# First mixture of a two-block kernel: one gather for two experts, results spread by 32-row strips, and layer one's further passes behind its whole first pass

## The reference, cut to what matters

```
logits = h @ w_router + b_router
top_v, top_e = top_k(logits, 4);  weights = softmax(top_v)
# for each expert e, with the tokens routed to it:
hcat  = x[tok] @ w1[e] + b1[e]                  # 1024 -> 2048
x_glu = min(hcat[:, ::2], 7);  x_lin = clip(hcat[:, 1::2], -7, 7)
act   = x_glu * sigmoid(1.702 * x_glu) * (x_lin + 1)
y     = act @ w2[e] + b2[e]                     # 1024 -> 1024
out[tok] += weights[tok, e] * y
```

## Time and profile before

| what | us |
|---|---|
| median of 3 runs | 2179.35 |
| the runs | 2178.27 to 2183.54 |
| span of the profiled execution, core 0 | 2180.7 |
| first mixture in it: first layer one to the last sum | 392.4 to 1397.5 |
| tensor engine busy | 1818.2 (83%) |

### The profile page before, as it was taken

How to read it: one execution, slowest core, us unless ns; L and a number is a source line. 1 busy time by engine, 2 the same in 40 slices (tenths; PEclk the granted TensorE clock), 3 DMA queues, 4 the chain that set the end, 5 groups by cost and what they waited for, 6 DMA issues and landing times. The chain is left out here.

```text
span 2180.7 us, 28331 instructions
## 1 busy us (share of the span) xinstructions
PE 1818.2 (83%) x11496; PEld 831.2 (38%) x11496; DVE 806.8 (37%) x1613; ACT 506.2 (23%) x1028; POOL 77.0 (4%) x96
## 2 busy tenths in 40 slices
PE   7899999999999988989977898599989855565556
PEld 3654445433333433434333243255534522222221
DVE  2215533333342434534444344488882200000001
ACT  2022311232331233332333333222410200000000
POOL 0000000000000000000000000085000000000000
PEclk9999999999999999999999999799999878877888
DMA  7835349789897799999999999534228299999997
GB/s 268 301 133 195 136 173 376 316 367 409 342 420 311 309 425 423 422 423 402 425 422 423 423 424 423 189 121 142 91 102 345 96 429 428 427 428 428 428 427 320
DMA packets 114821, 713.56 MB, mean 327 GB/s; under 512 B 16799, under 2 KB 21102, under 8 KB 69006
## 3 DMA queue, kind: packets, MB, share of 16 engines
q1 hardware_dynamic: 106208, 704.98, 79.3%
q10 hardware_dynamic: 8398, 5.47, 0.9%
HBM read 709.35 MB, written 1.07 MB: 326 GB/s over the span
## 5 line engine op out<-in xcount | busy, mean ns | idle before, releaser
L881 PE MATMUL ps<-ring,ar 128*32 128x512 f32 x3072 | 368.3, 620 | 41.7 <-DMA ring<-in_w 18.4
L481 PE MATMUL ps<-ar 128*128 128x128 f32 (+5 forms) x1742 | 351.2, 359 | 41.0 <-PEq L755 20.5
L488 PE MATMUL ps<-ring,ar 128*32 128x512 f32 x1184 | 196.0, 691 | 138.0 <-DMA ring<-in_w_gate 45.3
L481 PEld LDWEIGHTS ps<-ar 128*128 128x128 f32 (+2 forms) x1742 | 234.1, 200 | 160.5 <-issue 121.8
L481 PE MATMUL ps<-ring,ar 128*128 128x512 f32 (+2 forms) x592 | 248.8, 580 | 3.8 <-DVE ar L1423 1.7
L881 PEld LDWEIGHTS ps<-ring,ar 128*32 128x32 f32 x3072 | 99.3, 113 | 307.5 <-issue 279.9
L1825 DVE TENSOR_SCALAR ar<-ps 128x256 f32<-128x256 f32 x128 | 54.4, 425 | 403.8 <-PE ps L881 395.0
L893 PE MATMUL ps<-ring,ar 128*32 128x512 f32 x1536 | 175.0, 602 | 0.0
L596 PE MATMUL ps<-ring,ar 128*128 128x512 f32 x384 | 170.2, 594 | 0.0
L481 PEld LDWEIGHTS ps<-ring,ar 128*128 128x128 f32 x592 | 113.2, 193 | 132.8 <-issue 127.0
L2400 ACT ACTIVATE ar<-ps 64x512 f32<-64x512 f32 x256 | 151.3, 591 | 46.6 <-PE ps L893 33.4
(11 more groups left out here) (403 smaller groups left out, 1385.8 us busy)
## 6 DMA issues: line engine op xcount, KB each, us to landing
ring<-in_w SPq DMA_DIRECT2D x192, 2048.0 KB, 20.0
ring<-in_w_gate SPq DMA_DIRECT2D x25, 2048.0 KB, 29.4
ring<-in_w_up SPq DMA_DIRECT2D x25, 2048.0 KB, 31.4
ring<-in_w_down SPq DMA_DIRECT2D x24, 2048.0 KB, 30.1
ring<-in_w_in SPq DMA_DIRECT2D x21, 2048.0 KB, 8.7
ring<-in_w_ada SPq DMA_DIRECT2D x12, 2048.0 KB, 8.5
ar<-in_w_up SPq DMA_DIRECT2D x7, 2048.0 KB, 29.2
ar<-in_w_gate SPq DMA_DIRECT2D x7, 2048.0 KB, 29.6
```

What stands on the lines that cost most here:

```text
L481: ins = self.t.e.matmul(o, l, r, start=(i == 0), stop=(i == len(pairs) - 1))
L488: ins = self.t.e.matmul(b[32 * i:32 * i + 32, :], l, r, start=(k == 0), stop=(k == len(steps) - 1))
L881: ins = e.matmul(b[32 * s:32 * s + 32, :], HG[:, 2 * c + r, 32 * n:32 * n + 32], W[:, r, HALF(s)], start=False, stop=(c == 3 and r == 1))
```

## The change

- **Gather.** The tokens of experts u and u+1 (the first 64 of each) are gathered together (`gather_pair`), every second expert, again with 32 instructions of 128 columns. For an expert with over 64 tokens the others are gathered inside its condition (`rest`: 16 products of 64 columns for the tokens, 16 of 32x128 for the selection), before its second pass. The selection of each expert is turned for 64 tokens by 16 products in column strips (`turned_picks`) where four transposes stood.
- **Layer one.** The first pass runs over c0 and c1, then expert u-1 is spread, then c2 and c3. All further passes follow in one condition. The four w1 slots are freed behind it.
- **Layer two.** A pass is 32 products of 256 columns, where it was 16 of 512, each strip of 32 output rows holding a quarter of the width. The second pass's activations are turned between its halves. One buffer of turned activations is left of two.
- **Spread.** A pass of expert u-1 is 8 products with 32 rows and 256 columns, the four row strips side by side, into four banks. The passes beyond the first are in conditions. DVE then adds four 128x512 sums, whatever the count.
- **ACT** copies 128x256 once per pass out of layer two, where it copied 64x512 twice.

The core of the diff of the tensor engine's program (the second mixture's functions are only renamed by it):

```diff
+    def turned_picks(t, b, u, passes):
+        for i, n in enumerate(passes):
+            for tb in range(2):
+                for q in range(4):
+                    ins = t.e.matmul(b[32 * q:32 * q + 32, TB(2 * i + tb)], SWB[u % 2][:, tb, 32 * n:32 * n + 32],
+                                     ident, start=True, stop=True)
+        return ins
+    def gather_pair(t, w, p, h, lane):
...
+        for k in range(4):
+            n = w.sums(b[:, TB(k)], [(XNV[:, tb, TB(4 * h + k)], SB[p % 2][:, :, tb, 0:64]) for tb in range(2)])
...
         def spread1(u, count):
-            spread(t, w, 1, u, TL1)
...
+            def rows(n):
+                t.wait_ge(s_act, act["yg", 1, u, n])
+                for tb in range(2):
+                    for q in range(4):
+                        g = slice(32 * q, 32 * q + 32)
+                        ins = e.matmul(banks4[q][:, 256 * tb:256 * tb + 256], SWT[u % 2][g, n, TB(tb)], YG_[g, n, :],
+                                       start=(n == 0 and tb == 0), stop=True, skip_group_check=True)
+                return ins
...
-            for half in range(2):
-                pe["l1", u, half] = t(layer1(b0, 0, half, True))
...
-                either(t, x, count, 32, second)
-                for c in (2 * half, 2 * half + 1):
-                    w.free("w1", u, c)
...
+            def third():
+                t.wait_ge(s_act, act["rest", u])
+                only(t, count, 96, lambda: layer1(w.claim("l1", u, 3, lane=(3,)), 3, (0, 1, 2, 3), False))
+                layer1(w.claim("l1", u, 2, lane=(2,)), 2, (0, 1, 2, 3), False)
+            def second():
+                either(t, (r,), count, 64, rest)
+                b1 = w.claim("l1", u, 1, lane=(1,))
+                layer1(b1, 1, (0, 1), False)
+                only(t, count, 64, third)
+                x(layer1(b1, 1, (2, 3), False))
+            pe["l1", u, 0] = t(layer1(b0, 0, (0, 1), True))
             if u > 0:
                 spread1(u - 1, counts[u - 1])
+            pe["l1", u, 1] = t(layer1(b0, 0, (2, 3), True))
...
+            either(t, (x, r), count, 32, second)
+            pr["rest", u] = r.n
+            for c in range(4):
+                w.free("w1", u, c)
...
+            b = w.claim("l2", u, 0, lane=(7,))
+            layer2(b, 0, (0,), True, None)
+            turn_act(1, (1,), 5)
+            pe["l2", u, 0] = t(layer2(b, 0, (1,), True, first_second))
```

More of the change, by code:

```diff
@@ L826, in tensor_moe1 @@
         tensor_route(t, w, 1, WR1, 32, 128)
-        gather_rows(t, w, 1, 0, TL1)
-        gather_weights(t, w, 1, 0, TL1)
+        for h in range(2):
+            gather_pair(t, w, 0, h, (TL1[h],))
+        gather_turned(t, w, 0, (6,))
         tensor_ada(t, w, 5, 1)
@@ L878, in layer1, with layer2 @@
                     W = RG_(slot["w1", u, c], 0, 2, 2048)
-                    for r in range(2):
+                    for r_ in range(2):
                         for s in range(4):
-                            ins = e.matmul(b[32 * s:32 * s + 32, :], HG[:, 2 * c + r, 32 * n:32 * n + 32],
-                                           W[:, r, HALF(s)], start=False, stop=(c == 3 and r == 1))
+                            ins = e.matmul(b[32 * s:32 * s + 32, :], rows_of(2 * c + r_, n),
+                                           W[:, r_, HALF(s)], start=False, stop=(c == 3 and r_ == 1))
                 return ins
-            def layer2(b, n, arrive, first):
+            def layer2(b, n, halves, arrive, first):
                 for s in range(4):
+                    if s // 2 not in halves:
+                        continue
                     if arrive and s % 2 == 0:
@@ L933, in tensor_moe1, with rest, third @@
-            px["l1", u] = x.n
+            def rest():
+                b = w.claim("hr", u, lane=(3,))
+                for k in range(8):
+                    for tb in range(2):
+                        e.matmul(b[:, 64 * k:64 * k + 64], XNV[:, tb, TB(k)], SB[u // 2 % 2][:, u % 2, tb, 64:128],
+                                 start=(tb == 0), stop=(tb == 1))
+                b = w.claim("sr", u, lane=(2,))
+                r(turned_picks(t, b, u, (2, 3)))
+            def third():
+                t.wait_ge(s_act, act["rest", u])
+                only(t, count, 96, lambda: layer1(w.claim("l1", u, 3, lane=(3,)), 3, (0, 1, 2, 3), False))
+                layer1(w.claim("l1", u, 2, lane=(2,)), 2, (0, 1, 2, 3), False)
@@ L1132, in tensor_moe2 @@
         tensor_route(t, w, 2, W36, 36, 32)
-        gather(t, w, 2, 0, TL2)
+        gather(t, w, 0, TL2)
         for u in range(NE // 4):
@@ new lines, in scalar_rest @@
+    def scalar_rest(s, u):
+        s.wait_ge(s_pr, pr["rest", u])
+        if u > 0:
+            s.wait_ge(s_px, px["l1", u - 1])
+        if u > 1:
+            s.wait_ge(s_pe, pe["sp", 1, u - 2])
+            s.wait_ge(s_ps, psp[u - 2])
+        s(s.own.activation(HGR, ps("hr", u).rearrange("p (k s) -> p k s", k=8), ACT.Copy))
+        read["hr", u] = s.mark()
+        act["rest", u] = s(s.own.activation(SWT[u % 2][:, 2:4, :], ps("sr", u).rearrange("p (n q) -> p n q", n=2),
+                                            ACT.Copy))
+        read["sr", u] = s.mark()
@@ L2360, in scalar_gather_rows, with scalar_gather_weights, scalar_gather @@
+    def scalar_gather_weights(s, u):
+        s.wait_ge(s_pe, pe["swt", 2, u])
+        if u > 1:
+            s.wait_ge(s_pe, pe["sp", 2, u - 2, 0, 1, 1])
+        s(s.own.activation(SWT2[u % 2][:, 0:1, :], ps("swt", 2, u)[:, 0:256].rearrange("p (i q) -> p i q", i=1),
+                           ACT.Copy))
+        read["swt", 2, u] = s.mark()
+    def scalar_gather(s, u, l1):
+        scalar_gather_weights(s, u)
         for h in range(2):
-            if h == 1 and between is not None:
-                between()
@@ L2373, in scalar_moe1 @@
+            read["hg", 2, u, h] = s.mark()
+        act["hg", 2, u] = n
     def scalar_moe1(s):
```

349 lines of the change are left out of this document (172 added, 177 removed).

## The result

| what | before | after |
|---|---|---|
| median of 4 runs, us | 2179.28 | 2347.84 |
| the runs, us | 2178.27 to 2183.54 | 2344.24 to 2351.05 |
| span of the profiled execution, us | 2180.7 | 2343.6 |
| last product of layer one (T), us | 1372.2 | 1541.0 |
| last sum of the first mixture, us | 1397.5 | 1559.4 |

The ratio is 1.076, interval 1.074 to 1.078. The prediction said 2176, from 2164 to 2190, and was wrong by far. The loss lies ahead of T (168.8 us), and the end behind it became shorter, by 6.9 us.

A forecast was written before the change was run, and what follows sets the result against it. The prediction took weight transfers at 421 GB/s to bound the first mixture from 752 us on; 2180.7 + 3 (release) + 4 (stalls) - 10.5 (end) = 2177.2 profiled, so 2176 us as median, range 2164 to 2190.

The forecast's parts named there:

- The bound: First mixture, 752 to 1345 us: weight transfers bound the kernel, at 421 GB/s and 5.0 us each.
- four stretches: Before 752 us, transfers below 421 GB/s lose 13.5, 7.9, 10.7 and 28.7 us, in all 61.
- the covers: Four transfers still ahead when an expert's c3 has landed, 19.9 us; one-pass and two-pass experts were taken as covered.
- Stalls inside the holds: Waits on issue, behind conditions and half clock while w1 slots stay held: 0 to 12 us, taken as +4.
- five holds: Delays from c3's landing to the slots' release at the five three-pass experts (2, 4, 8, 9, 18).
- the hold is longer: Rival: three-pass experts' holds exceed the cover by more; 3 us more a hold is +15, 2191; chance 0.2.
- Part 1, the engine's work: Gather, spread, selection and rest on the tensor engine: relieved of about 113 us, most beside transfers and worth nothing by itself.
- Part 2, the release: Later freeing of layer one's w1 slots: transfers lose 64 us against 61, so +3.
- the filling: The ring's first filling, at expert 0: slots free later, the loss growing to 13.5 + 7.8 = 21.3 us.
- the long hold of an expert with three passes: From c3's landing 22.4 us, 26.2 to the next transfer's start; transfers stop 6.3 us at each such expert.
- Part 3, the end: Chain from layer one's last product to the last sum: T + 16.1 or 12.8 against 25.3; gain 9.2 to 12.5, taken as -10.5.
- The clock: Rival: more idle on the tensor engine lowers its clock; further passes at 0.8 lengthen each hold by 4 us, 2192; chance 0.05.

The follow-up runs named there:

- w96: The changed kernel without the fourth pass, with layer two and spread products of 512 columns again (spread in two 64-row strips); 2214.2 us, ratio 1.0155.
- c_late: b_cap96 with all four w1 slots freed behind the whole of layer one, where two were freed behind each half; 2159.3 us, ratio 0.9906.
- b_cap96: The kernel before without the fourth pass (tokens over 96, which no expert here has), on all engines; 2157.8 us, ratio 0.9890.
- b_dead: The kernel before with 92 and 48 never-made products per expert inside conditions of layer one's second half and layer two; 2404.8 us, ratio 1.1017.
- b_strewn: The kernel before with 140 never-made products per expert in seven separate conditions of 20; 2340.2 us, ratio 1.0720.
- a_halves: The changed kernel with layer one's further passes in two conditions again, two w1 slots freed behind each; 2322.0 us, ratio 1.0654.

## Why the prediction was wrong

**The bound.** Right for before: weights, 421 GB/s, 61 us lost in four stretches (63 by the landings). But it took the covers for safe. The one-pass experts had 21 us of work in 29.8 of transfers, and the change put 12 us of waiting and half clock into each. The step that failed is that no term asked what the 21 one-pass experts pay. The prediction costed passes that are made, and a pass that is not made at nothing. The change lengthened the conditions of the two layers from 160 to 240 products (32 for 16 in each further pass of layer two, and `rest`), that of the spread from 4 to 24, and made one condition of layer one's two. That was read off nowhere, though the diff shows it.

**"Stalls inside the holds", +4 (0 to 12).** This was the only term for the waits behind L755 and on issue, and it looked for them in five holds. They were at nearly every expert. 58.9 us of them in before grew to 215.3. The earlier trace rows showed the start of it: 12.3 and 10.7 us at L881, 23 us without a semaphore or a transfer behind them, which should have been followed to their other places (20.5 us at L481 by the list of waits) and asked for their cause. The rival "the hold is longer" names new code fetched inside a condition among its causes; its place was wrong (five experts with three passes) and its price too (+15).

**Part 1, the engine's work, -113.** The durations were right where the clock is full: `rest`'s gather 3.79 us (3.7 forecast), the selection 1.08 (1.0), layer two 1.93 for each half. From the start of a spread pass to the next product are 1.07 us (0.95), and 0.86 for each further pass. The sum nearly arrived as work and not as time. In the first mixture of before the engine was busy for 899 us, 72 of them at half clock, and after for 893, of which 253 at half clock. At full clock that work would be 864 and 767 us, 97 less where 113 were forecast. But the page's busy time fell by 5 us, since behind the waits the engine ran at half clock. Layer one alone, with the same instructions as in the earlier trace rows, shows it:

```profile
L922 PE MATMUL ps<-ring,ar 128*32 128x512 f32 x3072 | 402.2, 664 | 10.7 <-issue 10.5
```

402.2 against 368.3, 34 us for the same work.

**Part 2, the release, +3.** The mechanism was right and could be seen once the code was short: the filling shifted by 7.9 us (c2 of expert 1 lands at 418.2, before at 410.3; 7.8 forecast), and w96's idle stretches stand at the forecast experts, in sum 67 us against 43. That the later release costs little by itself is right by c_late, which has no loss that can be told from b_cap96, but also not the long hold of an expert with three passes. No kernel shows the price of that hold apart from the jumps'. In the changed kernel the same four sites lost 99, since experts 2, 4, 8 and 18 each began with a wait of 4.8 to 5.3 us behind a jump, which the forecast holds did not have.

**Part 3, the end, -10.5 (9.2 to 12.5).** Mis-sized. In order of time, to be held against the earlier trace rows:

```profile
1537.38 3.64 PE L922 MATMUL ps<-ring,ar 128*32 128x512 f32 x32
...
1544.46 0.41 PE L949 MATMUL ps<-ar 128*128 128x128 f32 x2 [3.44 <-DVE ar L1885]
...
1545.34 3.44 PE L936 MATMUL ps<-ring,ar 128*32 128x256 f32 x32 [0.47 <-ACT ar L2504]
...
1549.21 1.93 PE L936 MATMUL ps<-ring,ar 128*32 128x256 f32 x32
...
1553.93 1.15 PE L869 MATMUL ps<-ar 32*128 32x256 f32 x16 [2.79 <-ACT ar L2504]
...
1556.50 2.87 DVE L1819 TENSOR_TENSOR ar<-ps,ar 128x512 f32<-128x512 f32 x4 [3.02 <-PEq L758]
```

From T = 1541.0 to 1559.4 are 18.4 us, a gain of 6.9. Layer two ended at T + 10.1 (10.4 forecast). Behind it the engine waited 2.79 us until ACT had copied the result (a copy of 0.8 was forecast there; ACT, still at the other passes, began it 1.9 us after layer two's end), and DVE's sums were released by a condition's end (PEq L758) 1.4 us behind the last product of the spread. So it was T + 18.4 for T + 16.1.

**The rivals.** None gave the result. "The clock" (0.05) was right in its mechanism, the idle gaps did bring half clock, but it placed it in the holds. The chances were spread over variations of one picture, in which the slots and the covers decide, and the range of 26 us held no case in which the engine's own sequence of instructions becomes the bound.

## What to carry to other kernels

Count the code that a condition passes over, not only the work that it makes: here jumps over up to 160 instructions were free in two kernels that had no longer ones and little code in all (b_cap96, c_late), and jumps over 384 or more behind layer one cost 3 to 5 us nearly every time. In the changed kernel a further 3 us at half clock followed. An edit that saves executed work by more and smaller instructions in passes that are seldom made can be a loss, and leaving out the code of a pass that the input never needs was worth 20 us in the kernel before. When a profile shows waits on issue or behind a condition's end, without a semaphore or a transfer, follow them before anything else: they grow with the code, and no cover was meant for them.

## What was not expected of the hardware

- Products that never execute cost 221 us, when 140 of them were added to the code of each expert (b_dead).
- The instruction packets follow the code's volume: 71 more in b_strewn, for 560 instructions added to each expert, and 28 fewer in b_cap96, for 54 products (216 instructions) taken out, both some 250 instructions a packet. Code that is passed over is fetched too.
- A wait behind a jump lasted 6.2 us with the weights' transfers at full rate (b_dead, 431 GB/s meanwhile; the longest was 6.7, in a_halves), though a packet is in the trace for about 1 us. How much of the rest is queueing behind the weights was not tried.
- Row strips run side by side better when there are four of them: 16 instructions of 32 rows and 256 columns took 1.15 us (L869 above), where 16 of half the columns take 1.87 one after another (3.74 for 32). The two strips of 64 rows and 512 columns in w96 took 1.99 us for 8 instructions.
